# Four units of 896 columns per expert in the first mixture, weights loaded in halves

## The reference, cut to what matters

```python
combine = ...                      # per token: two of eight experts, softmax weights
for e in range(8):                 # wg, wu: [1024, 3584]; wd: [3584, 1024]
    he = silu(t @ wg[e]) * (t @ wu[e])
    out = out + (combine[:, e:e + 1] * he) @ wd[e]
```

## Time and profile before

| | |
|---|---|
| time, median of three runs | 2470.89 us |
| the profiled execution: its own time, its span | 2475.48 us, 2473.7 us |
| TensorE (PE) busy | 2396.1 us, 97% of the span |
| VectorE, ScalarE, GpSimd busy | 632.1, 305.5, 157.8 us |
| first mixture, first `up` to last `down` | 458.1 to 1391.4 us of the span |
| matmuls of `up` (L791), busy | 590.6 us |
| matmuls of `down` (L806), busy | 300.5 us |
| bytes read from memory over the span | 674.09 MB |

### The profile page before, as it was taken

One profiled execution on the slowest core, in us unless ns is written; L12 is line 12 of the kernel. 1 busy time (PEld: TensorE's weight loads), 2 busy tenths in 40 slices (PEclk: granted clock), 3 DMA queues, 4 the chain that ended last, 5 costly groups with the idle time before them and its releaser, 6 DMA issues.

```text
span 2473.7 us, 51664 instructions
## 1 busy us (share of the span) xinstructions
PE 2396.1 (97%) x24104; PEld 1539.6 (62%) x24104; DVE 632.1 (26%) x1139; ACT 305.5 (12%) x510; POOL 157.8 (6%) x173
## 2 busy tenths in 40 slices
PE   7999999999999999999999899989999999999998
PEld 5647777766666666666666587887668654444443
DVE  1640002201011111011010136561525242223223
ACT  1220000100000000000000133221323110000000
POOL 2000000000000000000000002531202000000000
PEclk9999999999999999999999989899999999999999
DMA  8693434699999999999999600012124469999995
GB/s 324 239 339 138 152 103 147 246 394 367 392 368 394 368 394 368 384 376 368 393 368 393 251 1 1 1 66 105 69 87 154 170 241 428 430 428 428 429 428 237
DMA packets 216969, 678.55 MB, mean 274 GB/s; under 512 B 5908, under 2 KB 9455, under 8 KB 204335
## 3 DMA queue, kind: packets, MB, share of 16 engines
q1 hardware_dynamic: 214320, 669.01, 70.1%
q0 software_dynamic: 2112, 6.05, 0.7%
q10 hardware_dynamic: 318, 0.10, 0.0%
HBM read 674.09 MB, written 1.05 MB: 273 GB/s over the span
## 4 chain that ended last, share of the span: by engine, by line
PE 83%; DVE 6%; DMA 6%; issue 2%; ACT 1%; SPq 1%; POOL 0%; POOLq 0%; DVEq 0%; ACTq 0%
PE ps L669 24%; PE ps L791 21%; PE ps L806 9%; PE ps L882 9%; DMA ring<-in_moe_wd 6%; PE ps L902 5%; PE ps L1085 3%; PE ps L869 2%; SPq L534 1%; PE ps L1240 1%; ACT arena L2300 1%; PE ps L1414 1%; PE ps L1419 1%; PE ps L769 1%; PE ps L1250 1%
## 5 line engine op out<-in xcount | busy, mean ns | idle before, releaser
L791 PE MATMUL ps<-ring,arena 128*32 128x256 f32 x10752 | 590.6, 379 | 0.5 <-DVE arena L1958 0.5
L791 PEld LDWEIGHTS ps<-ring,arena 128*32 128x32 f32 x10752 | 348.5, 110 | 232.6 <-issue 2.7
L669 PE MATMUL ps<-hT,ring 128*128 128x256 f32 (+1 forms) x1680 | 398.9, 397 | 0.0
L669 PEld LDWEIGHTS ps<-hT,ring 128*128 128x128 f32 x1680 | 320.4, 191 | 81.3 <-issue 42.1
L2300 ACT ACTIVATE arena<-ps 128x512 f32<-128x512 f32 (+5 forms) x238 | 117.1, 523 | 1722.2 <-PE ps L791 781.5
L806 PE MATMUL ps<-ring,arena 128*32 128x256 f32 x5376 | 300.5, 379 | 2.5 <-DMA ring<-in_moe_wd 2.4
L806 PEld LDWEIGHTS ps<-ring,arena 128*32 128x32 f32 x5376 | 173.9, 110 | 118.3 <-DMA ring<-in_moe_wd 4.1
L1640 DVE TENSOR_TENSOR arena<-arena,ps 128x384 f32<-128x384 f32 x56 | 31.0, 554 | 592.5 <-ACT arena L2300 592.5
L882 PE MATMUL ps<-ring,arena 128*64 128x512 f32 x672 | 146.9, 592 | 0.0
L2683 POOL TENSOR_SCALAR small<-small 128x1 f32<-128x1 f32 x18 | 6.1, 340 | 1919.5 <-ACT arena L2300 1919.3
L669 PE MATMUL ps<-arena 128*128 128x128 f32 (+1 forms) x1032 | 122.1, 276 | 6.6 <-ACT arena L2300 2.5
(11 more groups left out here) (387 smaller groups left out, 2034.3 us busy)
## 6 DMA issues: line engine op xcount, KB each, us to landing
ring<-in_moe_wg SPq DMA_DIRECT2D x56, 2048.0 KB, 12.6
ring<-in_moe_wu SPq DMA_DIRECT2D x56, 2048.0 KB, 17.7
ring<-in_moe_wd SPq DMA_DIRECT2D x56, 2048.0 KB, 19.0
ring<-in_w_exp_up SPq DMA_DIRECT2D x22, 2048.0 KB, 17.0
ring<-in_w_exp_down SPq DMA_DIRECT2D x22, 2048.0 KB, 19.9
ring<-in_w_exp_gate SPq DMA_DIRECT2D x20, 2048.0 KB, 17.2
ring<-in_w_in SPq DMA_DIRECT2D x14, 2048.0 KB, 9.1
ring<-in_w_ada SPq DMA_DIRECT2D x12, 2048.0 KB, 13.5
```

Source lines behind the costliest of these rows:

```text
L669: last = mm(outp, l, r, start=(i == 0), stop=(i == n - 1))
L791: last = mm(o_, x_[:, k, 32 * r:32 * r + 32], gu[:, :, k, :, q, :], start=(k == 0), stop=(k == KC - 1))
```

## The change

The unit grows from 512 to 896 columns: four units an expert, 32 in all. One unit's weights now fill the whole ring, in six parts. wg and wu come in halves of four row blocks each: slots 0 and 1 hold row blocks 0 to 3 of wg and wu, slots 2 and 3 row blocks 4 to 7 (1.835 MB a slot, pieces of 3584 bytes). The 896 rows of wd are laid out with seven neighbouring rows on a partition: slot 4 holds the first four of each seven (2.097 MB, pieces of 16 KB), slot 5 the last three (1.573 MB, pieces of 12 KB). Each part has its own semaphore (`m1_uh`, `m1_up`, `m1_dh`, `m1_dn`) and is asked for again, for the next unit, when its one slot has been read. `up` runs over row blocks outside and token groups inside, with 448 moving columns a matmul: 192 instructions a unit as before, half of them for each half of the weights. `down` has seven blocks, 96 and 72 instructions. VectorE's product is written in the order that the seven rows want (stride 7 in, runs out). PSUM banks 0 to 2 hold one token group each. Two of the six transposes of the gather move to banks 5 and 6, so `gathered` now waits for the transposes ahead of its copy, and ScalarE's second copy waits for that copy.

```diff
+UW1, QW, ROWS1 = 896, 224, 7
...
-        U1 = F1 // UW
+        U1 = F1 // UW1
...
+                def fetch_up(e, j, h, need):
+
+                    for t in range(2):
+                        s_ = 2 * h + t
+                        src = ins[("moe_wg", "moe_wu")[t]][0][e, 4 * h * P:(4 * h + 4) * P, j * UW1:(j + 1) * UW1]
+                        if need is not None:
+                            sp.wait_ge(*at(("m1_uh", "m1_up")[h], need))
...
+                def fetch_down(e, j, h, need):
+
+                    s_, b0, nb = 4 + h, 4 * h, (4, 3)[h]
+                    src = ins["moe_wd"][0][e, j * UW1:(j + 1) * UW1, :].rearrange("(p b) n -> p b n", b=ROWS1)[:, b0:b0 + nb, :]
+                    if need is not None:
+                        sp.wait_ge(*at(("m1_dh", "m1_dn")[h], need))
...
+                def expert(e, begin, end):
+
+                    for j in range(U1):
+                        n = R * UNITS + U1 * e + j
+                        if not (end and j == U1 - 1):
+                            for h in range(2):
+                                fetch_up(e + (j + 1) // U1, (j + 1) % U1, h, n + 1)
+                        if not (begin and j == 0):
+                            for h in range(2):
+                                fetch_down(e, j, h, n)
...
                     def up(j):
...
+                        for h in range(2):
+                            landed(2 * h, j)
+                            landed(2 * h + 1, j)
+                            gu = ring[:, 2 * h:2 * h + 2, 0:4 * UW1].rearrange("p m (k q n) -> p m k q n", k=4, q=4)
+                            for k in range(4):
+                                for r in range(3):
+                                    for q in range(4):
+                                        o_ = ps[32 * q:32 * q + 32, r, 0:2 * QW].rearrange("p (m n) -> p m n", m=2)
+                                        last = mm(o_, x_[:, 4 * h + k, 32 * r:32 * r + 32], gu[:, :, k, q, :],
+                                                  start=(h == 0 and k == 0), stop=(h == 1 and k == 3))
+                            last.then_inc(inc(("m1_uh", "m1_up")[h]), 1)
...
                     def down(j):
...
+                        for h in range(2):
+                            landed(4 + h, j)
+                            nb = (4, 3)[h]
...
+                            last.then_inc(inc(("m1_dh", "m1_dn")[h]), 1)
...
                 def gathered(g, b):
                     ve.wait_ge(*at("m1_gath", KC * (R * G_ + g) + KC))
-                    if x == "x":
-                        ve.wait_ge(*at("m1_gcd", R * G_ + g + 1))
+                    ve.wait_ge(*at("m1_gcd", R * G_ + g + 1))
                     copy(xgT[:, b, 0:KC * C1].rearrange("p (k c) -> p k c", k=KC)).then_inc(inc("m1_xg"), 1)
...
-                        V.tensor_tensor(un_act, un_sg, up_, ALU.mult).then_inc(inc("m1_act"), 1)
+                        V.tensor_tensor(un_act.rearrange("p r (b i) -> p r b i", b=ROWS1), rows_first(un_sg), rows_first(up_), ALU.mult).then_inc(inc("m1_act"), 1)
...
-                    act(un_GcT[:, b, 4:6, :].rearrange("p i q -> p (i q)"), ps[:, 2, 0:2 * P], ACT.Copy).then_inc(inc("m1_gcT"), 1)
+                    ac.wait_ge(*at("m1_xg", R * G_ + g + 1))
+                    act(un_GcT[:, b, 4:6, :], ps[:, 5:7, 4 * C1:4 * C1 + P], ACT.Copy).then_inc(inc("m1_gcT"), 1)
```

More of the change, by code:

```diff
@@ L300, in build @@
         xnA = xn
[L301 to L303 removed]
+        un_sg = area(2048, 3, QW)
+        un_actT = area(11600, 3, ROWS1, 32)
+        un_act = area(12288, 3, QW)
         un_Gc = area(13056, NT, 3, 4, 32)
@@ L537, in gate_up @@
[L537 to L571, removed]
+                def fetch_up(e, j, h, need):
[4 more added lines that the diff above has]
+                            sp.wait_ge(*at(("m1_uh", "m1_up")[h], need))
+                        elif first[s_]:
+                            sp.wait_ge(*at(first[s_][0], first[s_][1]))
+                        sp.dma_start(ring[:, s_, 0:4 * UW1].rearrange("p (k n) -> p k n", k=4), src.rearrange("(k p) n -> p k n", p=P))\
+                            .then_inc(inc("%sloaded%d" % ("" if x == "m" else "x1_", s_)), 16)
@@ new lines, in fetch_down @@
+                def fetch_down(e, j, h, need):
[3 more added lines that the diff above has]
+                        sp.wait_ge(*at(("m1_dh", "m1_dn")[h], need))
+                        if h == 0:
+                            sp.sem_inc(sem("m1_down_asked"), 1)
+                    elif first[s_]:
+                        sp.wait_ge(*at(first[s_][0], first[s_][1]))
+                    sp.dma_start(ring[:, s_, 0:nb * D].rearrange("p (b n) -> p b n", b=nb), src)\
+                        .then_inc(inc("%sloaded%d" % ("" if x == "m" else "x1_", s_)), 16)
@@ L573, in overflow_units @@
+                for h in range(2):
+                    fetch_down(0, 0, h, None)
+                expert(0, True, False)
+                with sp.Fori(1, E1 - 1) as e:
+                    expert(e, False, False)
+                expert(E1 - 1, False, True)
             def overflow_units():
@@ L642, in _ @@
             overflow_units()
-            before = [("m1_up", UNITS - 1), ("m1_up", UNITS - 1), ("m1_dn", UNITS - 1), ("m1_up", UNITS), ("m1_up", UNITS), ("m1_dn", UNITS)]
+            before = [("m1_uh", UNITS), ("m1_uh", UNITS), ("m1_up", UNITS), ("m1_up", UNITS), ("m1_dh", UNITS), ("m1_dn", UNITS)]
             for i in range(P2, M2):
@@ L783, in up @@
                             pe.wait_ge(*at("vc_kept", 2))
[L784 to L793, removed]
+                        for h in range(2):
+                            landed(2 * h, j)
[8 more added lines that the diff above has]
+                            last.then_inc(inc(("m1_uh", "m1_up")[h]), 1)
                     def down(j):
-                        w = b * U1 + j
-                        s_ = 3 * (w % 2) + 2
-                        pe.wait_ge(*at("%sloaded%d" % (ld, s_), (ld0 + h0 + w // 2) * 16 + 16))
                         pe.wait_ge(*at("m1_aT", n0 + j + 1))
@@ L801, in down @@
                             pe.wait_ge(*at("m1_added", (R * G_ + e) * 2 + 2))
[L802 to L809, removed]
+                        for h in range(2):
+                            landed(4 + h, j)
+                            nb = (4, 3)[h]
+                            d_ = ring[:, 4 + h, 0:nb * D].rearrange("p (b n) -> p b n", b=nb)
+                            for c in range(nb):
+                                for r in range(3):
+                                    for q in range(4):
+                                        last = mm(flat[32 * q:32 * q + 32, 3 * 512 + S * r:3 * 512 + S * r + S], un_actT[:, r, 4 * h + c, :],
+                                                  d_[:, c, q * S:(q + 1) * S], start=(j == 0 and h == 0 and c == 0 and r != 1),
+                                                  stop=(j == U1 - 1 and h == 1 and c == 2), skip_group_check=True)
+                            last.then_inc(inc(("m1_dh", "m1_dn")[h]), 1)
                     pe.wait_ge(*at("m1_xg", R * G_ + e + 1))
@@ L822, in units_round @@
                     for e in range(E1):
-                        expert(e, e % 2, U1 * e, U1 * (e // 2))
+                        expert(e, e % 2, U1 * e, U1 * e)
                 else:
@@ L826, in units_round @@
                         for b in range(2):
-                            expert(2 * p + b, b, R * UNITS + 2 * U1 * p + U1 * b, U1 * p)
+                            expert(2 * p + b, b, R * UNITS + 2 * U1 * p + U1 * b, 2 * U1 * p + U1 * b)
                 scatter(E1, 0)
```

26 lines of the change are left out of this document (11 added, 15 removed).

## The result

The changed kernel takes 2559.22 us, the median of four runs (2556.38 to 2564.64); the kernel before, in the same comparison, 2471.44 us. The ratio is 1.0354, with a 95% interval of 1.0333 to 1.0375: 88 us slower. The forecast was 2505 us, with a range of 2480 to 2526. The direction came true, the size did not.

The account below looks back on a forecast made before the run. TensorE was taken to bound the kernel by a hair, with the loads right behind. The terms -5.5 + 26 + 5 + 8 + 0.7 gave +34 us, 2505 us against the median, range 2480 to 2526.

Parts of the forecast that it names:

- step 4: Last `down` of an expert: C, queued behind A and B, comes 3.75 us late, +26 us over seven experts.
- lag: A load's time from issue to landing less its transfer; taken as 3.4 us, with ends 2.3 and 4.1.
- C and D: Loads of a unit's own wd: C the first part (4.89 us), D the last three rows (3.67 us, not late).
- A and B: Loads of the next unit's wg and wu: A the first halves, B the second halves, 9.0 us each.
- step 3: Loads in new sizes: 4.5 us a slot; a unit's bytes need 26.6 us against 27.1 of matmuls.
- Step 5: First unit of an expert: A for unit 1 starts on idle engines, 0.6 us late, 5 us in eight experts.
- Step 6: Clock falls after the long waits: 0 to 2 us a wait, taken as 1.1 for seven, 8 us in all.
- R2: Rival: C and A are late, but TensorE holds its clock: +26 us, 2497; chance 0.30.
- Steps 1 and 7: Step 1: larger matmuls gain 3.1 us; step 7: VectorE's longer work hidden, copy ahead of the first `up` +0.7 us.
- R1: Rival, not slower: C moves beside A and B, wait at the last `down` below 0.7 us, 2466; chance 0.08.
- R3: Rival: loads dearer (lag 4.1) and the clock falls each time: +57 us, 2528; chance 0.15.
- R4: Rival: short lag (2.3), cheap transfers, clock held: +12 us, 2483; chance 0.12.

Follow-up runs that it names:

- the first experiment: Changed kernel, with both wd loads of an expert's first unit issued ahead of the next unit's wg and wu loads: 2529.92 us, ratio 1.0228.
- the second experiment: As the first experiment, plus the fourth unit's wd loads issued between the two halves of the next expert's wg and wu: 2481.36 us, ratio 1.0036.
- the crossed order: Changed kernel, with an expert's last `down` moved behind the next expert's first `up`: 2500.04 us; with the scatter between the halves of up(1): 2467.91 us.
- the last gain of 0.26%: The crossed order with scatter between the halves of up(1), plus wd in 128-row blocks (4 KB pieces) and VectorE's product without stride: 2465.51 us, ratio 0.9974.

## Why the prediction was wrong

| step | forecast, us | measured, us |
|---|---|---|
| 1 and 2, matmuls and old waits | -5.5 | -5.5 (taken as forecast; an `up` 18.04 for 18.03, the old waits replaced) |
| 4, C late | +26 | +62.2 |
| 5, A of unit 1 late | +5 | +11.8 (1.7 of it in three waits for B) |
| 6, clock | +8 | +17.5 |
| 7, first copy | +0.7 | +0.7 (first `up` waits 1.21, before 0.53) |
| sum | +34 | +86.7 |

The spans differ by 89.1; 2.4 us are not assigned. From the first `up` to the end of the last `down` alone the difference is 88.2 us (1021.5 for 933.3), so the loss lies in this mixture.

**The step that failed is step 4**, in this sentence: "By the steps above the queue has about run dry when A is asked for." Its formula held. C late by lag + 0.35 gives 5.35 for the first expert (A's wg landed 9.5 us after issue, 5.0 beside its transfer) where 5.66 was measured, 8.75 for 9.43 in the second, and 5.75 for 6.09 in the first experiment. What is left over is about the 0.3 to 0.4 us from the end of a half `up` to the issue of A and the 0.14 from C landing to the matmul, which the formula has at nothing. What was wrong is the lag: 3.4 was taken, from engines that had fallen idle, and that is about what idle engines show here too (3.8). In the second expert it was 8.4. At A's request the engines were not idle, for two reasons.

The first, shown by the first experiment: C and D of an expert's first unit are held back behind A and B of unit 1 in SyncE's code. Step 4 looked at the fourth unit alone, where C's slot comes free last; it did not ask which load waits where its slot is long free. So some 16 us of the load engines' time go by unused in every expert from the second on, and C and D, 8.6 us by step 3, fall into the full stretch. The price is 16.5 us of waits.

The second: the queue does not work a backlog off from unit to unit. Step 3 had 26.6 us of loads against 27.1 of matmuls, and step 4 drew from them that the queue would be dry; half a microsecond of slack a unit against a backlog of several says the opposite. The changed kernel's trace shows it: in the second expert A lands 12.9, 12.1 and 12.9 us after issue for unit 2, for unit 3 and for the next expert. And the half microsecond itself was too much: in the third expert of the first experiment, where A of unit 2 found idle engines, a backlog came up anew, because the landings of A stood 28.1 and 27.9 us apart. Two slots issued together took 4.5 us each there too, so step 3 had the single transfers right, but the loads of a unit came in at longer intervals than their sum; why is open. From these late A come waits of 5.38 to 7.28 in the first experiment in place of 3.75 (45.7 us in place of 26), and they all but vanish once C goes ahead of B (3.4 us). That C stands behind A and B is thus shown to be the cause of this part, as the prediction said.

**Step 5** named place and cause, and was too small: 1.33 us in the second expert instead of 0.6. A on idle engines takes 8.3 + 4.5 = 12.8 us for both slots, not 12.4; it is issued 0.4 us after the half `up`, and the start of up(1) follows 0.14 us behind the landing. The price of the lag was taken from loads of other sizes. On SyncE's queue this load shows 3.8 us beyond the transfer. The Trainium skill (DMA: Bandwidth & Descriptors, Anatomy of one DMA) has about 2.0 us fixed a transfer, fitted on GpSimd's path; no load of this mixture goes by that path, and with its figure the forecast would have been further off. B was forecast as not late; three waits of 0.3 to 1.0 us for a B say otherwise.

**Step 6** had the fall of the clock and its range (0 to 2 us) from the earlier trace rows, where some of the matmuls were spread over idle time; and of those rows it counted only the stretch at 0.50, 1.4 us, while the next one, at 0.85 of the clock, adds about 0.45. In the changed kernel 2.5 us a wait were measured, over that range. The price did not grow with the wait: with wd in 4 KB pieces alone, waits of 6.17 to 10.77 us cost 1.4 to 2.2. R2, which held that dense matmuls around the wait keep the clock, is refuted for waits of 5.38 us and more: all fourteen such waits, in the changed kernel and the first experiment, were followed by a slow `down`. The Trainium skill (TensorE: Matmul & The Clock Gate, HAM oscillation) describes matmuls that pay behind each wait for a load; the trace agrees for these fourteen. Shorter waits did not always pay here: those up to 2.0 us left the clock at 1.00, and those of 2.52 us brought it down four times of eight.

**Steps 1 and 7** held, and of step 3 the single transfers: the `up` of 18.04 us, slots of 4.5 us, C 4.9 us behind the load ahead of it, the first `up`. (In the earlier trace rows the nines run to slice 22, not 21; nothing rests on it.) VectorE's product took 1.40 us, not 0.97, within the 1.9 that step 7 allowed for a slower stride, and covered.

**R1** would have C beside A and B; the second experiment, which changes nothing but the order of issue, shows that the order was at stake. R3, the dearest case, had the clock right in kind but looked for its loss in the price of a transfer, which was not it: a slot took the 4.5 us of step 3. R4's short lag of 2.3 us is nearly there once, in A of unit 2 of the first expert (7.0 us from issue to landing, 2.5 beside its transfer), but at no fourth unit.

## What to carry to other kernels

With one queue that issues in the order of the code, list for every load two times, when its slot comes free and when the waits ahead of it let it go; a load whose slot is free while the engines idle is worth moving up before anything else is sized. A rate just under the need is no slack: carry the backlog from stage to stage instead of assuming an empty queue. And a wait of TensorE as long as those that brought the clock down here (2.52 us in part, 3.52 us and more each time) is priced with the slow matmuls behind it, unless other useful work, here the next expert's first `up`, can be put into its place.

Not tried: the crossed order with the old units of 512 columns. So how much of the last gain of 0.26% comes from the larger matmuls and how much from the order is open.

## What the runs showed of the hardware

- The clock: after the eight equal waits of 2.52 us between matmuls of this mixture it fell four times, after none of the waits up to 2.0 us, and after all of 3.52 us and more. What decides at 2.52 us is open.
- A VectorE product of 128x672 in float32, read with a stride of seven elements, takes 1398 ns; without the stride 855.
- Issue to landing on idle load engines, from SyncE: 8.3 us in the second expert of the changed kernel for 1.835 MB, 3.8 beyond the transfer; 8.2 to 8.9 us at the same place in the six experts behind it.
